# One projection pass of each slot is issued ahead of that slot's output products and transposes

## What is computed

```
n   = RMSNorm(h)
q_A, k_A, v_A, q_B, k_B, v_B, gate_A, gate_B = split(n @ w_in)
o_A = dilated sliding-window attention, 8 heads of 64, softmax over the union of three patterns
o_B = stick-breaking attention, 8 heads of 64:
      z = q k^T / 8;  a = exp(log_sigmoid(z) + sum over later keys of log_sigmoid(-z));  o = a v
y   = (sigmoid(gate_A) * (o_A @ w_up_a) + sigmoid(gate_B) * (o_B @ w_up_b)) @ w_out
h   = h + y;  h = h + cross attention to 256 memory tokens;  h = h + SwiGLU(RMSNorm(h))
```

## Time and profile before

| | us |
|---|---|
| median of 3 runs | 1932.09 (1927.59 to 1935.17) |
| the profiled execution | 1938.46 |
| its span | 1936.7 |
| PE busy in the span | 1795.4 (93%) |
| DVE busy in the span | 989.0 (51%) |
| ACT busy in the span | 629.8 (33%) |

### The profile page before, as it was taken

The page is one execution under the profiler, slowest core; times in us unless marked ns, Lnnn a source line. Parts: engine busy times, 40 slices in busy tenths (PEclk is TensorE's granted clock), DMA queues, the critical chain, the costliest instruction groups (busy, mean ns, idle before and its releaser), DMA issues.

```text
span 1936.7 us, 24569 instructions
## 1 busy us (share of the span) xinstructions
PE 1795.4 (93%) x8610; PEld 1453.1 (75%) x8610; DVE 989.0 (51%) x1490; ACT 629.8 (33%) x1009; POOL 706.3 (36%) x848
## 2 busy tenths in 40 slices
PE   3799899989998999959999889999999999999996
PEld 3677677767776777748887767888888888888884
DVE  7345774677467765975444565323333332233236
ACT  4225664466456656753222333000000000000003
POOL 6632222222122221214454124444444444344445
PEclk8899999999999999979999889999999999999998
DMA  4311112101210111154312001111111111111112
GB/s 188 120 49 42 29 48 64 44 27 48 64 46 25 59 54 40 60 215 143 117 43 87 22 23 44 44 51 47 46 51 43 49 49 52 45 43 54 43 43 87
DMA packets 42201, 118.59 MB, mean 61 GB/s; under 512 B 5136, under 2 KB 13584, under 8 KB 42000
## 3 DMA queue, kind: packets, MB, share of 16 engines
q1 hardware_dynamic: 21312, 75.66, 11.8%
q10 hardware_dynamic: 20816, 41.95, 6.6%
HBM read 97.67 MB, written 18.87 MB: 60 GB/s over the span
## 4 chain that ended last, share of the span: by engine, by line
PE 76%; DVE 10%; issue 5%; ACT 5%; DVEq 0%; ACTq 0%; POOL 0%; DMA 0%; POOLq 0%
PE ps L385 65%; PE ps L531 3%; PE ps L494 3%; PE ps L508 2%; DVE e_row L1308 2%; DVE e_row L1305 1%; DVE rows L1317 1%; DVE pt L1328 1%; ACT pt L908 1%; DVE h L1549 1%; DVE raw L1215 1%; ACT e_row L893 1%; ACT e_row L895 1%; ACT n_hi L1026 1%; DVE rms L1420 0%
## 5 line engine op out<-in xcount | busy, mean ns | idle before, releaser
L348 POOL TENSOR_SCALAR w_hi<-w_stage 128x512 fp32r<-128x512 f32 x276 | 207.0, 768 | 1201.7 <-issue 640.7
L353 POOL TENSOR_TENSOR w_lo<-w_stage,w_hi 128x256 fp32r<-128x256 f32 x552 | 477.9, 897 | 11.5
L385 PE MATMUL ps<-n_hi,w_hi 128*128 128x512 f32 x1536 | 407.3, 407 | 38.0 <-DVE raw L1215 26.9
L385 PE MATMUL ps<-n_lo,w_hi 128*128 128x512 f32 x1536 | 387.6, 393 | 0.0
L385 PE MATMUL ps<-n_hi,w_lo 128*128 128x512 f32 x1536 | 385.7, 391 | 0.0
L385 PEld LDWEIGHTS ps<-n_hi,w_hi 128*128 128x128 f32 x1536 | 294.5, 195 | 106.2 <-DVE raw L1215 30.7
L385 PEld LDWEIGHTS ps<-n_lo,w_hi 128*128 128x128 f32 x1536 | 289.0, 189 | 60.6 <-issue 0.2
L385 PEld LDWEIGHTS ps<-n_hi,w_lo 128*128 128x128 f32 x1536 | 285.9, 188 | 58.6
L1409 DVE TENSOR_TENSOR h<-ps,h 128x512 f32<-128x512 f32 (+1 forms) x192 | 132.1, 691 | 159.9 <-PE ps L385 159.9
L1081 ACT ACTIVATE a_hi<-u_f 128x1024 fp32r<-128x1024 f32 x22 | 23.4, 1063 | 466.3 <-DVE u_f L1515 466.3
L1328 DVE TENSOR_TENSOR pt<-ps,pt 128x256 fp32r<-128x256 f32 (+3 forms) x96 | 91.9, 957 | 85.5 <-ACT pt L908 83.1
(11 more groups left out here) (175 smaller groups left out, 2183.4 us busy)
## 6 DMA issues: line engine op xcount, KB each, us to landing
w_stage<-weights_in SPq DMA_DIRECT2D x138, 512.0 KB, 3.3
gates_scratch<-raw ACTq DMA_DIRECT2D x16, 512.0 KB, 2.7
o_scratch<-o_sum ACTq DMA_DIRECT2D x64, 64.0 KB, 2.1
n_lo<-o_scratch ACTq DMA_DIRECT2D x8, 512.0 KB, 4.0
g_a<-gates_scratch ACTq DMA_DIRECT2D x8, 512.0 KB, 3.7
g_b<-gates_scratch ACTq DMA_DIRECT2D x8, 512.0 KB, 4.5
h<-x_t_in ACTq DMA_DIRECT2D x8, 512.0 KB, 7.2
out_t<-h ACTq DMA_DIRECT2D x16, 256.0 KB, 2.1
```

What stands on the lines that cost most here:

```text
L348: ins = pool.tensor_scalar(w_hi[:, b, at], stage[:, b, at], 1.0, 1.0, ALU.mult, ALU.mult)
L353: ins = pool.tensor_tensor(w_lo[:, b, at], stage[:, b, at], w_hi[:, b, at].bitcast(F32), ALU.subtract)
L385: ins = pe.matmul(bank, w[:, b, c:c + P], mv(k), start=(first and n == 0), stop=(last and n == total - 1))
```

## The change

In every slot the first entry of the plan that is a pass, and not a transposition of V, is issued right after `logits(s)`, before `attend(s - 4)` and `transposes(s - 3)`. Nothing is added or removed.

```
                 for s in range(SLOTS):
                     if s < N_CHUNKS:
                         logits(s)
+                    ahead = [n for n, (_, _, p) in enumerate(plan.fill[s]) if p is not None][:1]
+                    for n in ahead:
+                        fill(s, n)
                     if 0 <= s - LAG - 1 < N_CHUNKS:
                         attend(s - LAG - 1)
                     if 0 <= s - LAG < N_CHUNKS:
                         transposes(s - LAG)
-                    for name, half, p in plan.fill[s]:
...
+                    for n in range(len(plan.fill[s])):
+                        if n not in ahead:
+                            fill(s, n)
```

More of the change, by code:

```diff
@@ L537, in attend, with fill @@
                         ins.then_inc(av_full, 1)
+                def fill(s, n):
+                    name, half, p = plan.fill[s][n]
+                    if p is None:
+                        pe.wait_ge(bank_free, bank + (plan.units["V" + name[1]] + half + 1))
+                        q = query(s - LAG - 1)
+                        pe.wait_ge(o_sum_s, i * QUERIES + q)
+                        v_transposes(half, 6 + (q + 1) % 2)
+                    else:
+                        unit = plan.units[name] + half
+                        tile = W_MIX + HEAD_TILES + plan.tile[name]
+                        unit_pass(i * TILES_IN + (tile + 1), tile % 2, half, p, bank + (unit - 1))
                 for s in range(SLOTS):
```

## The result

| | before | after |
|---|---|---|
| median, us | 1933.63 (1927.59 to 1938.76, 4 runs) | 1986.51 (1983.70 to 1990.23, 4 runs) |
| the profiled execution, us | 1938.46 | 1987.44 |
| its span, us | 1936.7 | 1985.6 |

The change makes the kernel slower: the ratio is 1.0276, with an interval of 1.024 to 1.0311. The forecast was 1977, with a range of 1955 to 1997.

What follows compares the result with a forecast made beforehand. PE, busy 93% of the span, was taken to bound the kernel. Waits of 28.8 and 10.5 plus 6 for the clock made 45 over 1938.5, so 1983.8; less 6.4 for the median, 1977, range 1955 to 1997.

Steps and rivals of the forecast that it cites:

- the ring: In a slot, PE's transposes release, through ACT and DVE's `pt`, the read-out freeing the bank PE wants a few us later.
- P: How much later PE is than before at a place in the rounds; 0.65 at slot 9, 8.55 at slot 21.
- Waits for raw some 70: PE's waits for DVE's read-outs before passes p = 0 would go from 26.9 us in sum to some 70.
- Terms of waiting: Added delay from PE's waits in the rounds: 28.8 us in three looped rounds, 10.5 in the last, sum 39.3.
- whatever PE did before: Slot 15 of a looped round: the old wait of 6.47 ends with DVE, late by 3.21, so PE is 3.2 late.
- the prediction's clock term: Passes slowed by half clock behind new waits over 2 us, 1.7 each; 0 to 11.8 us, taken as 6.
- The upper bound of 11.8: Most that half clock could add: slots 13 and 16 of looped rounds, 6 and 15 of the last; 3 x 2.8 + 3.4.
- the busy term: Extra PE busy time in the rounds from passes at half clock behind the new waits, taken as 6 us.
- Swallowed: Slack of ACT and DVE takes up the 1.93 us delay in the rounds; 1940, range 1930 to 1950; chance 0.09.
- Faster: The moved pass covers waits of output products or transposes, 9 us at most; 1923; chance 0.05.
- Worse: All named passes slow, and further ones taken at full clock, so waits feed each other; 1993 and more; chance 0.08.
- either clock: The forecast itself, with full or half clock behind the new waits: 1962 to 1990, chance 0.78.

Runs made afterwards that it cites:

- the second pair: Kernels before and after, both unchanged, each run once more with a profile: 1927.78 us before and 1986.00 us after.
- the kernel without any wait for read-outs: The kernel before, with DVE's read-outs moved to the very start of its slot, ahead of row maxima and running sums: 1902.36 us.

## Why the prediction was right, point by point

**Direction and mechanism: right, and shown for about 40 of the 53 us.** That part of the cost runs through PE's waits for read-outs that stand behind `pt`. With the read-outs taken out of the ring the change costs 16 or 13.6 us instead of 53; moving passes in slots 16 and 17 alone makes the wait of 2.26.

**Places and sizes.** How much later the second round's logits come than before, counted from slot 1 (slot 0 ran partly at half clock in both, 8.94 us before and 8.05 after), beside the P of the prediction:

| logits of slot | predicted P | measured |
|---|---|---|
| 10 | 0.65 | 1.15 |
| 13 | 1.28 | 1.83 |
| 15 | 3.0 | 5.02 |
| 16 | 3.2 | 4.51 |
| 17 | 5.14 | 6.50 |
| 19 | 6.6 | 8.65 |
| 22 | 8.55 | 10.65 |
| next round | 9.6 | 13.14 |

- The waits came where they were forecast, and near their size: slot 9 0.54 (forecast 0.65), slot 12 0.32 (0.63), slot 13 2.63 (2.65), slot 16 2.26 (2.4), slot 18 1.26 (1.48), slot 21 3.82 (4.0), the last output product 1.01 (1.1); in the last round slot 6 2.12 (2.1) and slot 15 3.54 (3.7). Slots 9, 12 and 18 of the last round gave 1.75, 0.25 and 1.34, in sum 3.3 (3.5). The 0.89 of slot 14 has gone, and the 2.73 of the last round has become 1.18 with 0.64 before the logits.
- "Waits for raw some 70" was not the sum of its own terms: 26.9 + 3 x 9.3 + 9.3 are 64. Measured 60.2.
- Terms of waiting, 39.3 together: too large by 6 in the profiled pair. PE idles 33 to 34 us more there, 26 of them in the looped rounds (forecast 28.8) and 7 in the last (10.5). That last round still came 12.0 late, as PE was busy 4.6 longer in it; in the second pair it came 9.7 late, all of it waiting.
- Counted from slot 1, as in the table, the read-out of slot 12 came 3.8 late (forecast 3.2), the one of slot 16 5.6 (5.1).
- Slot 15 was forecast 3.2 late "whatever PE did before", as DVE works "without a gap". That held only where slot 13's pass ran at full clock: in the first round (2.11) slot 15's pass came 3.5 late, in the second and third (3.60 and 3.58) 4.7 and 4.8. Behind the slow pass slot 13's transposes came so late that DVE waited for their `pt`, which it had not done before (first row before, second after):

```profile
406.58 1.22 DVE L1328 TENSOR_TENSOR pt<-ps,pt 128x1024 fp32r<-128x1024 f32 x1
423.68 1.23 DVE L1336 TENSOR_TENSOR pt<-ps,pt 128x1024 fp32r<-128x1024 f32 x1 [1.00 <-ACT pt L916]
```

  So 1.2 to 1.4 of the 1.5 us got past slot 15's wait, near the 1.1 that the prediction's clock term has for slot 13.

**The mis-sized term is what PE loses while busy: 6 was taken, 15 was measured in the profiled pair and 21 in the second.** The upper bound of 11.8 was too low as well. For the passes that the prediction names (slots 13 and 16, slots 6 and 15 of the last round) the 6 was near: over 2.11 us each, they lost 6.0 us in the first execution of after and 7.3 in the second. The rest was put at nothing. In slot 21 the pass was slow in all three looped rounds (3.78), before in two of three: 2.0 more. The slow stretch does not always end with the pass: behind slot 21's, the logits of slot 22 (503.89 above) took 1.01 us and their mask 0.69; before, the pass was slow too, but these rows were

```profile
480.86 0.62 PE L494 MATMUL ps<-qk 64*128 64x256 f32 x6
481.41 0.44 PE L498 MATMUL ps<-mask_r,ident_r 128*128 128x128 f32 x2
```

which with 0.13 more in the pass makes 0.8 in the second round. And each boundary between a pass and small products costs some hundredths of a us: slots 7 and 10 of the second round, in whose passes there is no wait, took 5.97 and 6.39 us from logits to logits instead of 5.93 and 6.32, 0.04 and 0.07 more; over the slots of a round I estimate about 1 us from these two. Two small waits stood nowhere either: slot 10's logits waited 0.22 for the row maxima, and PE's idle time at the loop's start was 3.12 instead of 2.69. With the slow passes of slots 13 and 16 these are the parts by which the second round came 13.1 late instead of 9.6; against them stands slot 16, whose small products were slow before and no longer are (logits 1.01, now 0.62).

**Part of the hit is luck.** In the profiled pair the terms of waiting were 6 too large and the busy term 9 too small; the two errors cancel for the most part, and the sum of 45 stands beside 49 measured. Between the second executions of both kernels it was 58.

**The clock.** After the waits of 2.0 to 2.6 us both levels were seen, 2.11 and 3.60 us for the same pass in slot 13 of different rounds, so bounds on both sides were right; but of the twelve passes in slots 13 and 16 in the two executions of after, ten were slow at least for a part, so half was low for them. The section "HAM oscillation — how this bites in real kernels" of the Trainium skill's page "TensorE: Matmul & The Clock Gate" told the direction of this term: bursts behind waits begin at half rate. In that page's example the waits are of about 3 to 5 us, longer than the 2 us from which on the prediction applied it. The runs here agree for the waits of 6.1 to 7.5 us, each followed by a pass of 3.4 to 3.8, and only sometimes for those of 2.0 to 2.6.

**The median.** The profiled execution of before lay at the slow end of its spread, and the forecast took 6.4 off for it. The profiled execution of after (1987.44) lies within 1 us of its median, 1986.51: in it the slow passes are the rule. Of the 9.5 us by which 1977 missed, 3.6 are the sum's (1983.8 against 1987.4) and about 6 are this step's.

**The rivals.** *Swallowed* is out: DVE's gaps lie before `pt`, and the delay arrived behind them. *Faster* is out: the small waits in slot 14 did go, 0.89 each, and were paid back with 2.63 in slot 13. *Worse*: 1986.5 lies between the forecast's 1977 and its 1993, and nearer to 1993. With all named passes slow the forecast's own terms give 1932.1 + 39.3 + 11.8 = 1983, so the 1962 to 1990 given for "either clock" is wider than its terms, and the measured time lies above them. What *Worse* names, loss at places taken at full clock, did come, though it did not feed the waits: these stayed under their forecast.

**Open.** What decides which level of the clock a pass gets after a wait of about 2 us isn't settled; the same place of the same program shows both. Two further orders were not tried: by the kernel's code, transposes ahead of the output product would let ACT overwrite `pt` while it is read, and two passes ahead could let a p = 0 wait for a read-out that itself waits for transposes behind it.

## What to carry to other kernels

Before a wait is moved forward on an engine, follow what that wait's releaser waits for in its own queue: here PE's pass waited for DVE's read-out, which stood behind DVE's wait for PE's transposes of the same slot, so that work put ahead of the transposes came back to PE as a wait. The cure is in the other queue: a read-out that sets a bank free belongs ahead of the wait with which it has nothing to do, and that alone gave 29 us here (1902.36 against 1931.77). It has to stand where it delays nothing else that is waited for: directly ahead of `pt` it gave 13.5 us, at the slot's start 29. Filling in front of a wait helped in no run here, not even with the read-outs out of the ring; the order of three things (output product, pass, transposes) has to be judged by the distance from each producer to its consumer, as the kernel with the pass in the middle showed at 2006.

## What the runs showed of the hardware

- A wait of PE of about 2 us can, but need not, be followed by half clock. In the rounds of all profiled executions, 42 passes of eight matmuls stand behind waits of 1.87 to 2.65 us: 24 took 2.08 to 2.14 us, 18 took 2.57 to 3.78, the values between (3.04, granted clock 0.65) where only a part was slow. Of the 54 passes behind waits of 0.2 to 1.75 none was slow; of the 50 behind waits of 3.46 to 7.48 all were, at least for a part (2.67 to 3.78). This is not a bound for every wait: in slot 14 of the kernel with the read-outs ahead of `pt`, a wait of 1.57 us was followed by a granted clock of 0.62, and one of 1.59 in another round of it by none lower than 1.00. Three stretches of after show both levels and a mixture, slot 13 of the second round, slot 16 of the second, slot 13 of the first, each behind 2.3 to 2.6 us of waiting:

```profile
417.10:420.60 3.50, 3.50 (x9) 2.77 (x10) 1.69 (x2) 2.63 (x3) 0.00 (x0) 0.54 0.10 19
456.98:460.00 3.02, 3.02 (x10) 1.94 (x10) 2.58 (x4) 0.00 (x0) 2.29 (x3) 0.65 0.11 22
213.03:215.00 1.97, 1.97 (x9) 1.63 (x10) 0.18 (x1) 1.94 (x3) 0.00 (x0) 1.00 0.00 0
```

- The spread may go with it, which is argued and not shown: the kernel before, with such waits in each looped round, ran between 1927.6 and 1938.8 us, the kernel without any wait for read-outs between 1899.89 and 1902.86.
